# A decoder layer on one core: the turn of an attention step's output moved behind the next step's fourth scores

## The chip, the cores and the metric

The kernel runs on one core of a Trainium2 chip. The metric is the device time of one execution in microseconds (us); lower is better. A change of time is given against the kernel before.

## What is computed

One inference step of a one-layer decoder: a prompt of 512 tokens and 8 sample sequences of 8 tokens, model width 1024, in float32. The input projection gives q, k, v and two inputs of a convolution module. Attention has 8 heads of 64; the samples attend over a paged cache of 4096 keys each, in blocks of 256, of which the 3 with the highest mean score are taken besides the own one.

```python
z = h @ w_in + b_in
q, k, v, cva, cvg = jnp.split(z, [D_ATTN, 2 * D_ATTN, 3 * D_ATTN, 3 * D_ATTN + D_CV], axis=-1)
attn = moba_fn(q, k, v)
glu = cva * jax.nn.sigmoid(cvg)
c = _causal_dwconv(glu_ext, w_cv_dw, b_cv_dw)          # 31 taps
c = jax.nn.silu(_layernorm(c, g_cv_ln, b_cv_ln)) @ w_cv_pw + b_cv_pw
x = x + _rmsnorm(jnp.concatenate([attn, c], axis=-1) @ w_out, g_post_mix)
u = _causal_dwconv(ffn_hist + (_rmsnorm(x, g_pre_ffn) @ w_up), w_ffn_dw, b_ffn_dw)   # 3 taps
x = x + _rmsnorm((jax.nn.silu(gate) * val) @ w_down, g_post_ffn)
```

## The kernel before

Every engine runs its own instruction list, written out by hand in program order; semaphores join them. An engine never passes an instruction that waits, so the order in the code is the order on the engine.

After the input work the kernel goes through eight **steps**, b = 0 to 7, one for each sample sequence. A step has these parts, and the names are those of the code:

- **Scores.** `scores(b, j)`, j = 0 to 3, is TensorE's product of queries and a quarter of the keys (L520; the fourth also does the own keys, L532). The first two of a step run within the step before, behind its third and sixth `weigh`; the third and fourth stand at the head of the step. Each needs two tiles of keys that VectorE has turned (`turn_k`, L1372). ScalarE copies the scores out of the accumulator banks (`put_scores`, L1007), VectorE reduces them (`reduce_scores`, L1422 and L1423).
- **Softmax.** VectorE picks the blocks and adds the penalties (L1427 to L1456, among them L1435, L1439, L1442), ScalarE takes the exponentials (`exps`, L1013 and L1016).
- **The gap.** While VectorE and ScalarE do that, TensorE does other work: `glu_group` (L598) in steps 0 and 1, two tiles of the input projection in steps 2 to 4 (`TILES_IN`, `tile`, L611), statistics in step 5, nothing in step 6, `mix_half(1, ...)` of the output projection (L717) and `turn_history` (L728) in step 7.
- **Values.** `first_values` turns the probabilities (L553), then eight `weigh` (L574) multiply them with values that DMA brings; between these, `fill` puts more work of the projections and of the prompt's attention.
- **Output.** VectorE normalizes the step's output (`norm_out`, L1469 and L1473), which it can do only after the last `weigh`, and after everything that stands ahead of it in its own list, such as the turn of the next step's last keys and, in step 6, the rows of the residual (`mix_rows(0)`, L1534 to L1551). TensorE turns it (`turn_out`, L584), ScalarE copies it out (`put_out`, L1032). Only `turn_values`, `rows_out`, `first_values` and the end of the last step need that copy (semaphore `ot_put`).

Meanwhile ScalarE multiplies the taps of the 31-wide convolution (`taps`, L1072 and L1073), 24 in the eight `fill` of a step and up to 5 in its gap, and GpSimd adds each product to the sum (L1766). There are two product buffers, so neither gets far ahead. In step 7 ScalarE does a root, `row_root(0)` (L1208), at the head of the step; VectorE's `scale_rows(0)` (L1557, L1558) waits for it, and VectorE's scores of step 7 stand behind that.

Of the kernel before, what the change touches and what calls it, by code (L numbers as in the profile page):

```python
# [87 lines left out]
def build_layer(nc, a):  # L88
    ctx = ExitStack()
    with ctx:  # L90
# [361 lines left out]
        def _(pe):  # L452
# [359 lines left out]
            glu_group(0, 3)  # L812
            for b in range(NB):
                scores(b, 2)
                if b:
                    turn_out(b - 1)
                scores(b, 3)
                if b in (0, 1):
                    for n in range(4):
                        glu_group(2 * b + 1, n)  # L820
                if b in TILES_IN:
                    for x in TILES_IN[b]:
                        tile(x)
                    if b < 4:
                        turn_values(TILES_IN[b][0] // 2, b, True)
                if b == 4:
                    rows_out()
                if b == 5:
                    pe.wait_ge(s["o2_put"], 2)
                    statistics(conv, s["st1_done"], s["conv_done"], CT)  # L830
                if b == 7:
                    for n in range(4):
                        mix_half(1, n // 2, n % 2)
                    turn_history()
                if b in (2, 3):
                    pe.wait_ge(s["v2_home"], 2 * b - 2)
                if b == 7:
                    pe.wait_ge(s["hf_put"], 2)
                first_values(b)
                for u in range(SUPER):  # L840
                    weigh(b, u)
                    fill(b, u)
                    if b < NB - 1 and u in (2, 5):
                        scores(b + 1, u // 3)
# [110 lines left out]
        def _(act):  # L955
# [268 lines left out]
            for b in range(NB):  # L1224
                if b == 6:
                    roots_of_variance()
                put_scores(b, 2)
                if b:
                    put_out(b - 1)
                put_scores(b, 3)  # L1230
                if b in (0, 1):
                    gate_exp(2 * b + 1, 0)
                    gate_exp(2 * b + 1, 1)
                    taps(4)
                if b in TILES_IN:
                    taps(3)
                    put_tile(TILES_IN[b][0])
                    taps(2)
                if b == 5:
                    for half in range(2):  # L1240
                        act.wait_ge(s["st1_done"], half + 1)
                        act.activation(mu[:, half * HALF:(half + 1) * HALF], Z[half][:, 0:HALF], ACT.Copy,
                                       scale=1.0 / DA).then_inc(s["mu_put"], 1)
                if b == 7:
                    row_root(0)
                exps(b)
                if b in TILES_IN:
                    put_tile(TILES_IN[b][1])
                    if b < 4:
                        put_turned_value(TILES_IN[b][0] // 2)  # L1250
                if b == 4:
                    put_rows()
                    put_tails()
                if b == 7:
                    mix_squares(1)
                put_turned(b)
                if b < NB - 1:
                    spread_q(b + 1)
                for u in range(SUPER):
                    fill(b, u)  # L1260
                    if b < NB - 1 and u in (2, 5):
                        put_scores(b + 1, u // 3)
# [653 lines left out]
```

## Time and profile before

| | |
|---|---|
| time, median of 3 runs | 1134.69 us (1132.8 to 1135.31) |
| profiled execution: its time | 1133.18 us |
| profiled execution: its span | 1131.4 us |
| mean granted TensorE clock | 0.928 of full |
| busy: TensorE, VectorE, ScalarE, GpSimd | 964.3, 666.1, 443.9, 457.2 us |

The span is the profiled stretch from the first to the last instruction; the time is the same execution as the device measures it. Busy shares are a mean over stages that have different limits. The eight steps fill about 55 to 650 us, the feed-forward layer the rest.

### The profile page before, as it was taken

To read this page: it belongs to the slowest core of one execution; us is meant where nothing else is said; L and a number is where in the kernel's file an instruction comes from. 1 tells how busy PE (TensorE), PEld (TensorE's weight loads), DVE (VectorE), ACT (ScalarE), POOL (GpSimd) and SP (SyncE) were. 2 spreads that over 40 slices of the span, in tenths; PEclk is the share of its full clock that TensorE was granted. 3 is DMA by queue.
4 is the path that set the end of the run, shared out by engine and by line. 5 is a ranking of instruction groups with operands and counts; after the bars stand their busy time and mean duration, and the time that the engine had idled before them with its cause. 6 is when DMAs were issued, how large, how long until landed. Compare 5 with 4: busy or idle time off the path is not lost.

```text
span 1131.4 us, 19587 instructions
## 1 busy us (share of the span) xinstructions
PE 964.3 (85%) x7520; PEld 710.2 (63%) x7520; DVE 666.1 (59%) x928; ACT 443.9 (39%) x885; POOL 457.2 (40%) x408
## 2 busy tenths in 40 slices
PE   2498899787887695892988897999999999999995
PEld 1356675354453453552645557999999999767663
DVE  0758574554726456566444326988888888523214
ACT  1314655757656543434123213233333333224322
POOL 1002865839476432343000323555645655323440
PEclk9799998888899798997998898999999999999998
DMA  9688988979897765897871510322233231212222
GB/s 328 215 271 273 309 290 273 337 236 331 271 309 280 255 215 178 277 322 273 307 225 36 163 50 26 105 82 75 75 91 97 75 112 38 75 56 83 86 71 84
DMA packets 155207, 205.19 MB, mean 181 GB/s; under 512 B 10097, under 2 KB 75634, under 8 KB 155072
## 3 DMA queue, kind: packets, MB, share of 16 engines
q1 hardware_dynamic: 154619, 202.33, 54.2%
q10 hardware_dynamic: 495, 1.62, 0.5%
q8 instruction: 59, 0.97, 0.3%
q14 instruction: 34, 0.28, 0.1%
HBM read 198.59 MB, written 5.68 MB: 181 GB/s over the span
## 4 chain that ended last, share of the span: by engine, by line
PE 61%; DVE 13%; POOL 13%; ACT 7%; issue 4%; DMA 2%; POOLq 0%; SPq 0%; DVEq 0%; ACTq 0%
POOL conv L1766 10%; PE tp L857 6%; PE z L857 6%; PE sc L857 6%; PE z L717 4%; PE ob L857 3%; PE sm L857 3%; PE z L889 3%; PE ob L889 3%; PE tp L889 3%; PE z L598 2%; PE sc L520 2%; PE ob L574 2%; PE z L611 2%; DMA wk<-in_w_in 2%
## 5 line engine op out<-in xcount | busy, mean ns | idle before, releaser
L1766 POOL TENSOR_TENSOR conv<-conv,prod 128x576 f32<-128x576 f32 x120 | 170.3, 1419 | 106.4 <-ACT prod L1073 91.3
L1372 DVE STREAM_TRANSPOSE kT<-kN 128x2048 f32<-128x2048 f32 x64 | 145.4, 2295 | 29.0 <-PE sc L520 15.2
L1803 POOL TENSOR_TENSOR wulo<-wu,wuhi 128x2048 fp32r<-128x2048 f32 x22 | 102.6, 4662 | 24.4 <-ACT wuhi L1188 24.4
L1072 ACT ACTIVATE prod<-glu,consts 128x512 f32<-128x512 f32 x124 | 88.9, 717 | 47.7 <-POOL conv L1766 44.5
L1821 POOL TENSOR_TENSOR wdlo<-wd,wdhi 128x1024 fp32r<-128x1024 f32 x22 | 57.4, 2610 | 90.0 <-ACT wdhi L1303 90.0
L574 PE MATMUL ob<-vN,pT 128*32 128x128 f32 x2048 | 75.4, 296 | 15.4 <-DMA vN<-in_cache_v 15.3
L611 PE MATMUL z<-hT,wz 128*128 128x512 f32 x192 | 87.7, 613 | 0.0
L1698 DVE TENSOR_TENSOR cvo<-cvo,sg 128x576 f32<-128x576 f32 x22 | 85.0, 3862 | 0.0
L1673 DVE TENSOR_TENSOR fTlo<-fT,fThi 128x1152 fp32r<-128x1152 f32 x22 | 29.8, 1356 | 91.6 <-ACT fThi L1302 91.6
L574 PEld LDWEIGHTS ob<-vN,pT 128*32 128x32 f32 x2048 | 62.3, 143 | 30.7 <-DMA vN<-in_cache_v 16.8
L520 PE MATMUL sc<-kT,qS 128*32 128x256 f32 x1024 | 72.0, 429 | 5.4 <-DVE kT L1372 5.4
L1422 DVE TENSOR_REDUCE small<-S 128x8 f32<-128x512 f32 x32 | 21.6, 676 | 93.2 <-ACT S L1007 92.9
L1691 DVE SCALAR_TENSOR_TENSOR cvo<-ux,small,cvo 128x512 f32<-128x512 f32 x88 | 66.2, 752 | 3.1
L1799 POOL TENSOR_TENSOR h2lo<-h2raw,h2hi 128x512 fp32r<-128x512 f32 (+1 forms) x10 | 11.9, 1206 | 133.8 <-ACT h2hi L1215 133.8
L598 PE MATMUL z<-hT,wz 128*128 128x288 f32 x256 | 65.8, 416 | 0.0
L611 PEld LDWEIGHTS z<-hT,wz 128*128 128x128 f32 x192 | 37.1, 197 | 45.1 <-issue 44.8
L553 PE MATMUL tp<-consts,S 128*128 128x128 f32 x128 | 24.8, 358 | 42.9 <-issue 24.8
L1302 ACT ACTIVATE fThi<-fT 128x1152 fp32r<-128x1152 f32 x22 | 25.7, 1166 | 90.9 <-issue 86.6
L598 PEld LDWEIGHTS z<-hT,wz 128*128 128x128 f32 x256 | 49.0, 194 | 15.5 <-issue 2.1
L717 PE MATMUL z<-wo,hT 128*128 128x512 f32 x128 | 58.0, 605 | 0.0
L1839 POOL COPY last<-ux 128x2 f32<-128x2 f32 x44 | 9.7, 221 | 117.8 <-ACT ux L1286 117.8
L1777 POOL TENSOR_SCALAR pP<-pP,small 128x128 f32<-128x128 f32 (+3 forms) x32 | 34.1, 1083 | 54.1 <-DVE small L1515 54.1
(311 smaller groups left out, 2531.1 us busy)
## 6 DMA issues: line engine op xcount, KB each, us to landing
kN<-in_cache_k SPq DMA_DIRECT2D x256, 256.0 KB, 4.4
vN<-in_cache_v SPq DMA_DIRECT2D x256, 256.0 KB, 4.0
wu<-in_w_up SPq DMA_DIRECT2D x44, 512.0 KB, 4.6
wd<-in_w_down SPq DMA_DIRECT2D x22, 512.0 KB, 3.6
wz<-in_w_in SPq DMA_DIRECT2D x20, 512.0 KB, 6.6
wo<-in_w_out SPq DMA_DIRECT2D x1, 4096.0 KB, 14.2
wq<-in_w_in SPq DMA_DIRECT2D x1, 2048.0 KB, 15.1
wk<-in_w_in SPq DMA_DIRECT2D x1, 2048.0 KB, 19.8
```

Source lines behind the costliest of these rows:

```text
L520: ins = pe.matmul(bank[32 * h4:32 * h4 + 32, :].rearrange("p (a g k) -> p a g k", a=2, g=2)[:, :, g, :], qS[:, hc, :], kT[:, 2 * (j % 2):2 ...
L574: ins = pe.matmul(OB[32 * hp:32 * hp + 32, 0:P], w, vN[:, c % 4, i, hp * P:(hp + 1) * P], start=False, stop=(u == SUPER - 1 and i == 3))
L598: ins = pe.matmul(Z[half][:, 0:HALF], wz[:, i % 2, k, u, :], hT[:, k, half * HALF:(half + 1) * HALF], start=(k == 0), stop=(k == KC - 1))
L611: ins = pe.matmul(Z[x % 2][:, 0:TP_], wz[:, x // 2 % 2, k, x % 2, :], hT[:, k, 0:TP_], start=(k == 0), stop=(k == KC - 1))
L717: ins = pe.matmul(Z[nh][0:m, :], mixT[:, k, t * P:t * P + m], wo[:, k, nh * TP_:(nh + 1) * TP_], start=(k == 0), stop=(k == KC - 1))
L857: ins = pe.matmul(bank8[4 * (f % 2) + n][:, 0:HALF], w[:, k, u * P:(u + 1) * P], x[:, k, half * HALF:(half + 1) * HALF], start=(k == 0 and ...
L889: ins = pe.matmul(y_banks[nh][t][:, :], x[slot][:, k2, t * P:t * P + P], w[slot][:, k2, :], start=(kk == 0 and k2 == 0 and j == 0), stop=( ...
L1072: act.activation(dst[:, 0:TP_], glu[:, i, j:j + TP_], ACT.Copy, scale=w_cv[:, i, j:j + 1])
L1372: dve.transpose(kT[:, u % 4, :, :].rearrange("p c (i k) -> p i c k", i=4), kN[:, c % 3, :, :].rearrange("p i (c k) -> p i c k", k=32)).the ...
L1698: me3.then(dve.tensor_tensor(cvo[:, f % 2, 0, :], cvo[:, f % 2, 0, :], sg2[:, f % 2, :], ALU.mult))
L1766: ins = pool.tensor_tensor(conv[:, i, :], conv[:, i, :], prod[:, n % 2, :], ALU.add).then_inc(s["prod_used"], 1)
L1803: pool.tensor_tensor(wulo[f % 2][:, :, :], wu[f % 2][:, :, :, :].rearrange("p k u n -> p k (u n)"), wuhi[f % 2][:, :, :].bitcast(F32), ALU ...
```

## The change

`turn_out(b - 1)` moves on TensorE from between the third and the fourth scores to behind the fourth; in steps 1 to 4 it moves further, behind the first piece of the gap's work. ScalarE's `put_out(b - 1)` follows it. No instruction is added or taken away.

```diff
             for b in range(NB):
                 scores(b, 2)
-                if b:
+                scores(b, 3)
+                if b >= 5:
                     turn_out(b - 1)
-                scores(b, 3)
                 if b in (0, 1):
                     for n in range(4):
                         glu_group(2 * b + 1, n)
+                        if b and n == 0:
+                            turn_out(0)
                 if b in TILES_IN:
-                    for x in TILES_IN[b]:
-                        tile(x)
+                    tile(TILES_IN[b][0])
+                    turn_out(b - 1)
+                    tile(TILES_IN[b][1])
                     if b < 4:
                         turn_values(TILES_IN[b][0] // 2, b, True)
...
                 put_scores(b, 2)
-                if b:
+                put_scores(b, 3)
+                if b >= 5:
                     put_out(b - 1)
-                put_scores(b, 3)
                 if b in (0, 1):
                     gate_exp(2 * b + 1, 0)
+                    if b:
+                        put_out(0)
                     gate_exp(2 * b + 1, 1)
                     taps(4)
                 if b in TILES_IN:
                     taps(3)
                     put_tile(TILES_IN[b][0])
+                    put_out(b - 1)
                     taps(2)
```

TensorE's list at the head of step 7, as a piece of the difference; L584 is the turn of step 6's output, L717 the first of the gap's output projection:

```order
 L520 MATMUL sc<-kT,qS 32x2x128 [waits s_put,kt_ready]
 L520 MATMUL sc<-kT,qS 32x2x128 x15
-L584 MATMUL tp<-consts,oN 128x128 [waits o_norm]
 L520 MATMUL sc<-kT,qS 32x2x128 [waits s_put,kt_ready]
 L520 MATMUL sc<-kT,qS 32x2x128 x15
 L532 MATMUL sm<-kOwn,qS 32x64 x16
+L584 MATMUL tp<-consts,oN 128x128 [waits o_norm]
 L717 MATMUL z<-wo,hT 128x512 [waits t1_put]
 L717 MATMUL z<-wo,hT 128x512 x7
```

The turn, with its wait for the normalized output, now stands behind the fourth scores and still ahead of the projection.

ScalarE's list at the same place, before:

```order
L1203 ACTIVATE small<-small 128x1 [waits mo_sum]
L1007 ACTIVATE S<-sc 128x4x4x32 [waits scores_done]
L1032 ACTIVATE oT<-tp 128x128 [waits ot_done]
L1007 ACTIVATE S<-sc 128x4x4x32 [waits scores_done]
L1208 ACTIVATE small<-small 128x1 [waits x1_sq]
```

and of the change, where lines of ScalarE's code have a number higher by three:

```order
L1206 ACTIVATE small<-small 128x1 [waits mo_sum]
L1010 ACTIVATE S<-sc 128x4x4x32 [waits scores_done] x2
L1035 ACTIVATE oT<-tp 128x128 [waits ot_done]
L1211 ACTIVATE small<-small 128x1 [waits x1_sq]
```

The copy of the turned output now stands between the fourth scores' copy and the root, no longer ahead of that copy.

TensorE's list at the head of step 2, as a piece of the difference; the two groups of L611 are the gap's two tiles:

```order
 L520 MATMUL sc<-kT,qS 32x2x128 [waits s_put,kt_ready]
 L520 MATMUL sc<-kT,qS 32x2x128 x15
-L584 MATMUL tp<-consts,oN 128x128 [waits v2_home,o_norm]
 L520 MATMUL sc<-kT,qS 32x2x128 [waits s_put,kt_ready]
 L520 MATMUL sc<-kT,qS 32x2x128 x15
...
 L611 MATMUL z<-hT,wz 128x512 [waits z2_put,wz_full1]
 L611 MATMUL z<-hT,wz 128x512 x7
+L584 MATMUL tp<-consts,oN 128x128 [waits v2_home,o_norm]
 L611 MATMUL z<-hT,wz 128x512 [waits z2_put]
 L611 MATMUL z<-hT,wz 128x512 x7
```

Here the turn moved past the fourth scores and the first tile; steps 3 and 4 have the same. The lists of VectorE, GpSimd and SyncE are unchanged.

## Rows read from the trace of the kernel before

**Rows 1.** The page: the chain that ended last, shares by engine.

```profile
PE 61%; DVE 13%; POOL 13%; ACT 7%; issue 4%; DMA 2%; POOLq 0%; SPq 0%; DVEq 0%; ACTq 0%
```

**Rows 2.** Timeline, head of step 7: start us, us, engine line op; last idle before, releaser.

```profile
574.10 2.31 DVE L1372 STREAM_TRANSPOSE kT<-kN 128x2048 f32<-128x2048 f32 x1
...
579.25 1.91 PE L520 MATMUL sc<-kT,qS 128*32 128x256 f32 x32
...
585.08 0.35 DVE L1473 TENSOR_SCALAR oN<-ob,small 128x128 f32<-128x128 f32 x1
585.49 0.33 PE L584 MATMUL tp<-consts,oN 128*128 128x128 f32 x1 [4.33 <-DVE oN L1473]
585.75 3.48 PE L520 MATMUL sc<-kT,qS 128*32 128x256 f32 x32
585.85 0.28 ACT L1032 ACTIVATE oT<-tp 128x128 f32<-128x128 f32 x1 [3.54 <-PE tp L584]
...
589.27 1.09 ACT L1007 ACTIVATE S<-sc 128x512 f32<-128x512 f32 x1 [3.14 <-PE sc L520]
589.74 14.00 PE L717 MATMUL z<-wo,hT 128*128 128x512 f32 x32
590.16 0.25 ACT L1208 ACTIVATE small<-small 128x1 f32<-128x1 f32 x1
590.45 0.16 DVE L1557 RECIPROCAL small<-small 128x1 f32<-128x1 f32 x1 [5.01 <-ACT small L1208]
```

**Rows 3.** Chain that ended last, behind step 7's softmax: start us, us, what.

```profile
604.11 1.15 ACT t L1200 x4
...
717.26 6.40 PE tp L857 x48
```

**Rows 4.** Timeline, head of step 2.

```profile
210.44 2.31 DVE L1372 STREAM_TRANSPOSE kT<-kN 128x2048 f32<-128x2048 f32 x1
...
213.24 0.47 PE L584 MATMUL tp<-consts,oN 128*128 128x128 f32 x1 [5.08 <-DVE oN L1473]
...
217.36 1.08 ACT L1007 ACTIVATE S<-sc 128x512 f32<-128x512 f32 x1
...
218.23 0.32 ACT L1032 ACTIVATE oT<-tp 128x128 f32<-128x128 f32 x1
218.44 1.09 ACT L1007 ACTIVATE S<-sc 128x512 f32<-128x512 f32 x1
```

**Rows 5.** Timeline of GpSimd alone, gap of step 2.

```profile
220.32 4.50 POOL L1766 TENSOR_TENSOR conv<-conv,prod 128x576 f32<-128x576 f32 x3 [0.74 <-ACT prod L1073]
226.53 2.94 POOL L1766 TENSOR_TENSOR conv<-conv,prod 128x576 f32<-128x576 f32 x2 [1.71 <-ACT prod L1073]
```

**Rows 6.** Chain that ended last, gap of step 2.

```profile
222.05 3.06 DVE rank L1435 x2
...
226.66 1.32 DVE small L1442
```

**Rows 7.** Chain that ended last, steps 1, 5 and 6.

```profile
156.03 0.77 DVE rank L1435 x2
...
158.34 0.19 DVE small L1442
...
431.53 0.26 PE tp L584
...
439.48 4.32 DVE small L1442
...
506.12 3.75 DVE sd L1633
```

**Rows 8.** Stretches: busy us of PE, PEld, DVE, ACT, POOL; then clock, DMA share, GB/s.

```profile
586.40:589.00 2.60, 2.60 (x30) 1.33 (x26) 0.00 (x0) 0.00 (x0) 0.00 (x0) 0.50 0.07 9
...
302.70:309.50 6.80, 6.62 (x56) 5.47 (x57) 4.63 (x3) 5.43 (x13) 1.06 (x1) 0.50 0.38 127
```

**Rows 9.** Timeline of TensorE, `first_values` of step 3.

```profile
301.39 1.09 PE L553 MATMUL tp<-consts,S 128*128 128x128 f32 x8 [3.88 <-ACT vP L1054]
```

## The prediction

> **What bounds the kernel now.** I read the page first: TensorE is 61% of the chain that ended last, VectorE and GpSimd 13% each [rows 1]. That says little of a move inside a step, so I then followed the chain of work in order of time from 55 to 650 us, to see which engine carries it at the head of each step, and read the timelines there. The question at each head is the same: is anybody on the chain waiting for the fourth scores, which the turn of the output holds up?
>
> In step 7 the answer is yes. The last keys are turned by 576.4 us (574.10 + 2.31), and the third scores end at 581.16. The fourth could start then. In place of that TensorE stands 4.33 us at the turn, because VectorE normalizes the output only at 585.08. The fourth scores run from 585.75 and take 3.48 us where the third took 1.91. ScalarE copies them at 589.27, does the root L1208 at 590.16, and VectorE, idle for 5.01 us, goes on at 590.45 with what the root gives; its softmax stands behind that [rows 2]. Each of these is on the chain.
>
> In steps 2 to 4 the answer is no. TensorE waits for the output there too, 5.08 us in step 2, but nearly all of that it would wait for the keys anyhow: they are ready at 212.75 (210.44 + 2.31), 0.5 us before the turn. And ScalarE copies the third scores only at 217.36 and the fourth at 218.44, since it is held by the taps, at GpSimd's pace; the copy of the turned output sits between the two, at 218.23 [rows 4]. So the chain runs from GpSimd's sums over the third scores' copy to VectorE, and VectorE's reductions of the third scores cover the copy of the fourth. The timelines of steps 3 and 4 read the same, two repeats of the pattern.
>
> **Step 7, the main term.** Removed from the chain is what lies between the normalized output and the root. The turn goes on at 585.49 as before, since neither VectorE's list nor its inputs change; its copy starts at 585.85 and takes 0.28. The fourth scores now run at 581.2, take 1.9 us, and with the own keys end before 584; ScalarE copies them (1.09) by about 584.3, so it waits at the turned output as before. The root, third in line, comes right behind that copy. By the row of the root itself, which starts 0.20 us before its predecessor's 1.09 us run out (589.27 + 1.09 = 590.36 against 590.16), it would start at 585.85 + 0.28 - 0.2 = 585.95 to 586.1, where it started at 590.16. That is 4.1 to 4.2 us [rows 2].
>
> Does the second input keep up? The output projection in the gap, 14.00 us, starts at 589.74 now. It would start behind the turn, at 585.8, so 3.95 us earlier, and ends at 599.8. ScalarE's squares of its rows (L1200) start behind the exponentials; on the chain they stand at 604.11, so they would be ready for it at 599.9 [rows 2, 3]. The two shift by the same amount within 0.2 us. Should the clock be down, the projection is late. Today the granted clock is 0.50 of 2.4 GHz, its level of 1.2 GHz, during most of the fourth scores' 3.48 us [rows 2, 8]; the same 3.5 us over the projection would lose half of it, 1.7 us, and leave 2.5 us of the 4.2. Today 4.33 us of idleness lie ahead of that stretch; afterwards the wait is from 583.6 to 585.49, about 1.9 us, so the lower clock is less likely.
>
> Behind the gap everything hangs on engines, not on a fixed transfer: the chain goes over the squares, the history, `weigh` and the projections, and at 717.26 it is TensorE's up-projection without a break [rows 3]. The values for the first four `weigh` were issued before 583 us, the later ones are issued as `weigh` frees their buffers, and move along. The first load of up-weights waits for the own keys' scores and starts some 6 us earlier, into a stretch with free DMA. I let the gain through whole: **4.2 us**.
>
> **Steps 2 to 4.** ScalarE's copy of the turned output leaves its place between the two score copies: 218.44 - 218.23, some 0.2 us [rows 4]. The next taps start that much earlier, and GpSimd's three sums with them; they run 220.32 to 224.82 [rows 5]. VectorE's L1435, the pair, ends at 225.11, 0.3 us behind them, and takes 3.06 where the pair takes 0.77 in step 1 [rows 7]; L1442 ends at 227.98, when GpSimd's next sum ends (226.53 + half of 2.94 = 228.0) [rows 5, 6]. So VectorE's softmax is tied to GpSimd's sums and follows them. The second tie goes by the tile: the fourth scores start 0.87 us earlier, partly at the lower clock, the first tile ends 0.5 to 0.6 us earlier, ScalarE copies it, then does the moved copy (0.32 - 0.1), then the taps: a net 0.2 to 0.4 earlier. Gain per step 0.2 to 0.4, for three steps 0.6 to 1.2. I take 0.2 to 0.3 each, **0.7 us**, since the start of `first_values` and the tile behind it, both at the lower clock, pass on less than the whole.
>
> The moved turn itself costs 0.3 us of TensorE behind the first tile. It is hidden: TensorE is idle 3.88 us ahead of step 3's `first_values` [rows 9]. Without that cover it would be 0.3 us a step. `turn_values` waits for the copy and for the second tile; the copy is 7 us older.
>
> **Steps 1, 5, 6: nothing.** In step 1 VectorE's reduction of the fourth scores does not wait for its copy. In step 5 the chain does go over the turn, 0.26 us [rows 7], and that comes off; but VectorE's L1442 takes 4.32 us there where it takes 0.19 in step 1, until GpSimd's subtraction of the mean has ended, and this starts as before, with the statistics. The 0.26 us vanish in it. In step 6 VectorE does a 3.75 us reciprocal from 506.12 on [rows 7], while the fourth scores' copy is made in time.
>
> For L1442 the Trainium skill has a rule (SBUF — State Buffer, Who interferes with whom): VectorE's `tensor_scalar` in a two-port mode and GpSimd take one shared pair of ports, and the later one blocks until the other has finished. By the rule step 5 gains nothing; if VectorE were only slow in itself there, 0.26 us more would come off the sum. The row agrees with the rule: 4.32 us against 0.19.
>
> **Sum.** 4.2 + 0.7 = 4.9; less 0.4 for the chance (about one in four) that the projection loses 1.7 us to the clock: 4.5 us. Against the profiled execution's own 1133.18 us that is 1128.7. It lies 1.5 us below the median of the three runs; a median should come out at 1134.69 - 4.5 = **1130.2 us**. What a measurement of this kernel can tell from no change is about 0.2%, 2.3 us.
>
> **Rivals.**
> *The gain of step 7 is cut.* The clock is down during the projection, or the softmax is late for another reason, and 2.5 us remain; steps 2 to 4 give nothing, because the clock takes there what the copies give. For it speaks that `first_values` of step 3 starts at the full clock after 3.88 us of idleness and falls to 0.50 from 302.7 to 309.5 [rows 8, 9]; with 0.5 us more idleness ahead it may start at 0.50, which costs about half of the eight's 1.9 us. Time: 1134.69 - 2.5 + 0.9 = 1133.1.
> *No change at all.* The 4.2 us are given back behind step 7, at a transfer or another engine. Against it: from 617 us on no wait for a DMA stands on the chain. 1134.7.
> *Slower, by the clock.* Every moved wait changes the length of TensorE's pauses; if the lower clock covers more of the steps, each microsecond in it costs up to half a microsecond of TensorE. The stretch of step 3 is 6.8 us long [rows 8], up to 3.4 us of loss. Two such stretches more, in gaps that now run at the full clock, plus 3.4 us in the projection of step 7, cost 6.8 + 1.7 = 8.5 us against 4.9: 1138.3. It decides from about 10 us more at 0.50 on. Against it: no pause grows by more than 0.9 us, and the longest, in step 7, shrinks.
>
> On the clock the Trainium skill (TensorE: Matmul & The Clock Gate, HAM oscillation) says that waits of some length between bursts put the array back to half its clock, every time. By that rule a longer pause ahead of `first_values` speaks against the change, at up to 0.9 us in step 3, and the shorter one in step 7 for it, at 1.6 us. The trace shows both levels at these places.
>
> **Chances and range.** The forecast (gain of 3.3 to 6) 0.68; the cut gain (1 to 3.3) 0.17; no change 0.10; slower by the clock 0.05. The ends of the unknowns are 4.2 + 1.2 = 5.4 us and 2.5 - 0.9 = 1.6 us; with 1.2 us of spread as in the three runs, 1127.9 to 1133.2. Faster by over 0.2%: the forecast and most of the cut gain's upper half, some 0.78; within 0.2%: 0.17; slower: 0.05.
>
> **What the new profile would show.** At step 7's head the fourth scores right behind the third, 1.9 us for 32; the turn behind a wait of about 1.9 us; the root 0.1 us behind the turned output's copy and VectorE waiting for it under 1 us, not 5.01; the chain no longer over L520 between L584 and L1208; the projection's 32 in 14.0 us. At steps 2 to 4: ScalarE's two score copies back to back, L1435 and L1442 as long as before and 0.2 to 0.4 us earlier. Steps 5 and 6 unchanged, L1442 shorter by just the 0.26. Wrong it would be if the root still came late, if the distance from the root to `weigh` grew, or if the stretches at 0.50 grew by several microseconds.

## The result: 5 us faster, below the forecast range

The changed kernel takes 1127.15 us (median of 11 runs, 1124.76 to 1131.32). The kernel before, in 11 runs that belong to the same comparison (the three shown ahead of the prediction are among them), takes 1132.64 (1129.43 to 1135.31). The ratio is 0.9958, its 95% interval 0.9942 to 0.9974: a gain of 0.42%, 4.8 us of 1132.64 (2.9 to 6.6). The forecast was a gain of 4.5 us and a time of 1130.2, with a range from 1127.9. The gain came as forecast; the time lies 0.75 us below the range. Among the experiments further down two single executions ran far slower than all others, one of 3165.55 us of all_but_step7 and one of 1197.8 us of behind_first_piece; the medians of these two kernels count them, the ratios leave them out.

The profiled execution took 1130.34 us, span 1128.5 us, mean granted clock 0.931 (before: 1133.18, 1131.4 and 0.928).

The first part of the page to look at is the chain that ended last, which answers to [rows 1]:

```profile
PE 62%; DVE 13%; POOL 13%; ACT 7%; issue 3%; DMA 2%; POOLq 0%; SPq 0%; DVEq 0%; ACTq 0%
```

It can't tell the two kernels apart. The head of step 7 can. This is its timeline in the changed kernel, the piece that answers to [rows 2] (start us, us, engine line op; last the idle time before and its releaser). The numbers of TensorE's lines shown here are the same, ScalarE's have grown by 3, VectorE's and GpSimd's by 6:

```profile
579.79 3.64 PE L520 MATMUL sc<-kT,qS 128*32 128x256 f32 x64
...
583.49 1.10 ACT L1010 ACTIVATE S<-sc 128x512 f32<-128x512 f32 x1 [0.54 <-PE sc L520]
...
585.62 0.35 DVE L1479 TENSOR_SCALAR oN<-ob,small 128x128 f32<-128x128 f32 x1
...
586.02 0.33 PE L584 MATMUL tp<-consts,oN 128*128 128x128 f32 x1 [2.15 <-DVE oN L1479]
...
586.39 0.28 ACT L1035 ACTIVATE oT<-tp 128x128 f32<-128x128 f32 x1 [1.79 <-PE tp L584]
586.56 0.28 ACT L1211 ACTIVATE small<-small 128x1 f32<-128x1 f32 x1
...
586.88 0.16 DVE L1563 RECIPROCAL small<-small 128x1 f32<-128x1 f32 x1 [0.91 <-ACT small L1211]
```

The reader is to see three things. The third and fourth scores run as one group of 64 in 3.64 us, 32 in 1.8. TensorE still waits for the normalized output, but 2.15 us and not 4.33, and behind the scores. And the root L1211 comes 0.17 us behind the start of the turned output's copy, with VectorE waiting 0.91 us for it and not 5.01.

The two profiles are 0.54 us apart when the third scores start (579.25 and 579.79), so times are compared from there. The root starts 10.91 us behind that point before and 6.77 us now: **4.14 us earlier**.

What stands behind the root is less good. First the chain that ended last in the changed kernel (start us, us, what), then two stretches (busy us of PE, PEld, DVE, ACT, POOL; then clock, DMA share, GB/s) and TensorE's timeline at the projection's start:

```profile
586.02 0.33 PE tp L584
586.35 15.45 PE z L717 x32
...
601.82 0.69 ACT t L1203 x2
```

```profile
587.00:590.20 3.20, 3.20 (x5) 1.21 (x5) 3.13 (x6) 1.15 (x1) 0.00 (x0) 0.54 0.82 142
590.20:602.00 11.80, 11.80 (x32) 5.06 (x31) 7.80 (x25) 3.86 (x11) 0.00 (x0) 1.00 0.18 52
```

```profile
586.19 2.42 PE L717 MATMUL z<-wo,hT 128*128 128x512 f32 x3
```

From the turn to the squares the chain no longer goes over the softmax; it goes over the whole output projection. By TensorE's timeline this took 14.00 us before and takes 15.60 now (586.19 to 601.79): for 3.2 us the granted clock is 0.54, nearly its lower level of 1.2 GHz, and the first three matmuls need 0.81 us each. ScalarE's last squares end at 602.51 on the chain (601.82 + 0.69), 22.72 us behind the third scores' start. Before they end at 605.26 [rows 3], 26.01 us behind it. So the step gains **3.3 us** of the root's 4.14.

How long each step is can be read from one row per step, ScalarE's copy of the turned probabilities `pTo` (L1028; L1031 in the changed kernel). The changed kernel has it here for steps 6 and 7:

```profile
529.34 0.36 ACT L1031 ACTIVATE pTo<-sm 64x256 f32<-64x256 f32 x1
...
613.63 0.36 ACT L1031 ACTIVATE pTo<-sm 64x256 f32<-64x256 f32 x1
```

The distance is 84.29 us. The table gives these distances for all profiles; "step n" is the distance from the copy of step n-1 to that of step n.

| profile | step 1 | 2 | 3 | 4 | 5 | 6 | 7 |
|---|---|---|---|---|---|---|---|
| before | 61.0 | 68.4 | 64.9 | 69.3 | 78.9 | 75.3 | 87.5 |
| changed | 58.5 | 72.3 | 63.2 | 69.9 | 78.7 | 75.5 | 84.3 |
| only_step7 | 58.8 | 67.8 | 64.7 | 69.3 | 78.9 | 75.3 | 84.3 |
| all_but_step7 | 60.1 | 69.2 | 66.5 | 67.4 | 78.9 | 75.6 | 87.6 |
| norm_first | 60.5 | 68.9 | 65.0 | 69.4 | 78.9 | 75.3 | 82.1 |
| behind_first_piece | 60.3 | 66.3 | 65.0 | 69.0 | 78.8 | 75.6 | 82.1 |
| five_taps | 58.4 | 72.4 | 64.8 | 69.1 | 81.4 | 75.5 | 84.3 |
| direct_everywhere | 59.5 | 66.4 | 64.9 | 69.4 | 81.6 | 75.5 | 84.3 |
| step7_piece_only | 60.5 | 68.3 | 65.3 | 69.3 | 78.9 | 75.3 | 82.1 |
| norm_first_copy_behind | 61.0 | 68.8 | 65.0 | 69.3 | 78.9 | 75.3 | 82.1 |
| changed_again | 60.4 | 68.8 | 65.0 | 69.0 | 78.8 | 75.6 | 84.3 |
| norm_first_again | 61.1 | 69.4 | 63.8 | 69.5 | 79.0 | 75.3 | 82.1 |
| taps_behind | 60.5 | 67.3 | 64.2 | 68.8 | 78.7 | 75.5 | 84.3 |

Step 7 takes three values, 87.5, 84.3 and 82.1, and each is the same to 0.1 us in every profile of its kind. Steps 1 to 4 differ by up to 3.5 us between two executions of one and the same kernel (changed and changed_again, step 2), so a gain of tenths there can't be read from single profiles. From the last copy to the end of the span it is 515.0 us before (1131.4 - 616.38) and 514.9 in the changed kernel (1128.5 - 613.63): there nothing is given back behind step 7. In the five profiles in which step 7 takes 82.1 us it is 515.3 to 515.4, so some 0.4 us come back there.

Now steps 2 to 4. The chain in the gap of step 2, changed kernel, which answers to [rows 6] (L1441 was L1435, L1445 was L1439, L1448 was L1442), and GpSimd's timeline beside it, which answers to [rows 5]:

```profile
222.90 2.93 DVE rank L1441 x2
225.85 3.07 DVE rank L1445 x2
...
229.66 0.19 DVE small L1448
```

```profile
221.02 7.60 POOL L1772 TENSOR_TENSOR conv<-conv,prod 128x576 f32<-128x576 f32 x5 [0.59 <-ACT prod L1076]
```

Before, GpSimd made three sums, stood idle 1.71 us and made two more. Now it makes five without a break, since the first tile is copied out early enough for ScalarE's next taps. VectorE's two rank pairs both stand in that stretch, and each takes 3 us where it takes 0.8 without a sum beside it. The forecast had only L1441 wait. L1448 is free in return: 0.19 us where L1442 took 1.32. From the start of the first pair to the end of L1448 it is 6.95 us where it was 5.93, so 1.0 more. In step 5 the chain goes over the scores as one group, without the turn between them, and L1448 is hardly longer than before (4.32 us [rows 7]):

```profile
430.22 3.63 PE sc L520 x64
...
439.63 4.37 DVE small L1448
```

### The profile page after: what moved, and what is told of

Its sections match the earlier page's. It is cut to its first block, busy times and chain, and to the rows that moved or that the text cites. A ratio compares the mean times of both kernels' runs of the same rounds, so it can differ in the third digit from the quotient of the medians.

```text
span 1128.5 us, 19587 instructions
## 1 busy us (share of the span) xinstructions
PE 959.1 (85%) x7520; PEld 708.5 (63%) x7520; DVE 670.4 (59%) x928; ACT 444.7 (39%) x885; POOL 459.9 (41%) x408
## 4 chain that ended last, share of the span: by engine, by line
PE 62%; DVE 13%; POOL 13%; ACT 7%; issue 3%; DMA 2%; POOLq 0%; SPq 0%; DVEq 0%; ACTq 0%
POOL conv L1772 10%; PE tp L860 6%; PE z L860 6%; PE sc L860 6%; PE z L717 5%; PE ob L860 3%; PE sm L860 3%; PE z L892 3%; PE ob L892 3%; PE tp L892 3%; PE z L598 2%; PE sc L520 2%; PE z L611 2%; PE ob L574 2%; DMA wk<-in_w_in 2%
## 5 line engine op out<-in xcount | busy, mean ns | idle before, releaser
L1704 DVE TENSOR_TENSOR cvo<-cvo,sg 128x576 f32<-128x576 f32 x22 | 93.8, 4265 | 0.0
L574 PE MATMUL ob<-vN,pT 128*32 128x128 f32 x2048 | 74.4, 293 | 17.2 <-DMA vN<-in_cache_v 17.2
L611 PE MATMUL z<-hT,wz 128*128 128x512 f32 x192 | 86.8, 606 | 0.0
L574 PEld LDWEIGHTS ob<-vN,pT 128*32 128x32 f32 x2048 | 61.4, 142 | 32.3 <-DMA vN<-in_cache_v 19.3
L520 PE MATMUL sc<-kT,qS 128*32 128x256 f32 x1024 | 67.9, 413 | 11.2 <-DVE kT L1378 11.2
L611 PEld LDWEIGHTS z<-hT,wz 128*128 128x128 f32 x192 | 36.2, 194 | 43.6 <-issue 43.4
L717 PE MATMUL z<-wo,hT 128*128 128x512 f32 x128 | 59.6, 619 | 0.0
L520 PEld LDWEIGHTS sc<-kT,qS 128*32 128x32 f32 x1024 | 34.0, 118 | 38.5 <-issue 12.0
```

The lines of the kernel that those rows point to most:

```text
L520: ins = pe.matmul(bank[32 * h4:32 * h4 + 32, :].rearrange("p (a g k) -> p a g k", a=2, g=2)[:, :, g, :], qS[:, hc, :], kT[:, 2 * (j % 2):2 ...
L574: ins = pe.matmul(OB[32 * hp:32 * hp + 32, 0:P], w, vN[:, c % 4, i, hp * P:(hp + 1) * P], start=False, stop=(u == SUPER - 1 and i == 3))
L611: ins = pe.matmul(Z[x % 2][:, 0:TP_], wz[:, x // 2 % 2, k, x % 2, :], hT[:, k, 0:TP_], start=(k == 0), stop=(k == KC - 1))
L717: ins = pe.matmul(Z[nh][0:m, :], mixT[:, k, t * P:t * P + m], wo[:, k, nh * TP_:(nh + 1) * TP_], start=(k == 0), stop=(k == KC - 1))
L1704: me3.then(dve.tensor_tensor(cvo[:, f % 2, 0, :], cvo[:, f % 2, 0, :], sg2[:, f % 2, :], ALU.mult))
```

## The experiments

Theory A, from the trace: the whole gain is step 7's; of it the root gives 4.1 us and the lower clock over the projection takes 0.8 back. Its rival B: steps 2 to 4 give a part as forecast, and it is only not seen in single profiles. Eleven runs followed, ten of nine edited kernels and one of the changed kernel again; all ratios are to the kernel before on the same chip.

### The two halves of the change

**only_step7**: the change in step 7 alone.

```diff
                 scores(b, 2)
-                if b:
+                if 1 <= b < 7:
                     turn_out(b - 1)
                 scores(b, 3)
+                if b == 7:
+                    turn_out(b - 1)
```

(and the same for `put_out` on ScalarE.)

> The kernel before with the turn of step 6's output alone moved behind step 7's fourth scores; steps 1 to 6 as before. Theory (the gain is step 7's): 3.2 to 4.2 us faster than before, ratio 0.9963 to 0.9972, and within 1 us of the whole change; VectorE's wait for the root under 1 us, the projection in the gap on the chain if the clock is down. Rival (the gain is in steps 1 to 4, step 7 is given back later): within 1 us of before.

**all_but_step7**: the changed kernel, with step 7 as before.

```diff
                 scores(b, 2)
+                if b == 7:
+                    turn_out(b - 1)
                 scores(b, 3)
-                if b >= 5:
+                if b in (5, 6):
                     turn_out(b - 1)
```

(and the same for `put_out` on ScalarE.)

> The whole change except step 7, whose turn stays between third and fourth scores. Theory: steps 2 to 4 give between 1 us and nothing, since GpSimd's sums block VectorE's L1439 for some 2.3 us whenever the first tile ends before ScalarE asks for it, and give 0.2 to 0.4 us when it doesn't: ratio 0.999 to 1.001. Rival: 2 to 4 us faster, ratio 0.9965 to 0.998.

Measured: only_step7 1128.61 us (12 runs), ratio 0.9965 (0.9951 to 0.998); all_but_step7 1132.53 us (12 runs), ratio 0.9999 (0.9987 to 1.0011); the kernel before 1133.17 (29 runs). Theory A holds. The moves of steps 1 to 6 together are worth nothing that can be measured; by the interval it is at most 1.5 us of gain and at most 1.2 of loss.

### The wait at the turn, and the projection's clock

If the projection loses 1.6 us because TensorE stands at the turn just ahead of it, then a kernel in which it doesn't stand there should reach more than the change. Two ways: make the output ready earlier, or put work ahead of the turn.

**norm_first**: the kernel before, with all turns in their old places; VectorE alone normalizes step 6's output ahead of the residual's rows.

```diff
-                    elif u == 7:
-                        mix_rows(0)
...
                 norm_out(b)
+                if b == 6:
+                    mix_rows(0)
```

> The kernel before with another edit: VectorE normalizes step 6's output ahead of the residual rows mix_rows(0) and no longer behind them; the turn stays between third and fourth scores. If the turn's wait for the normalized output is the cause, this alone removes it: 4.0 to 4.6 us faster than before (ratio 0.996), the turn without a wait, the projection starting near 584 and not on the chain. If it was only the place of the turn or of its copy that cost (the rival), nothing changes.

Measured: 1126.73 us (6 runs), ratio 0.9946 (0.9928 to 0.9963); and again on another chip, as norm_first_again:

> VectorE normalizes step 6's output ahead of the residual's rows, all turns where they stood before; once more, beside the changed kernel on the same chip. If the two microseconds of step 7 by which it is ahead in the profiles (82.1 against 84.3) are real, it comes out at 0.994 to 0.995 of the kernel before and 1.5 to 2 us under the changed kernel. If they are lost in later waits, the two are equal within 0.7 us.

1127.04 us (6 runs), ratio 0.9946 (0.9925 to 0.9968). The timeline of norm_first_again at the head of step 7, and the stretch of the projection in which the changed kernel has the clock at 0.54:

```profile
579.73 1.91 PE L520 MATMUL sc<-kT,qS 128*32 128x256 f32 x32
...
580.19 0.35 DVE L1473 TENSOR_SCALAR oN<-ob,small 128x128 f32<-128x128 f32 x1
...
581.57 0.33 PE L584 MATMUL tp<-consts,oN 128*128 128x128 f32 x1
...
581.83 1.93 PE L520 MATMUL sc<-kT,qS 128*32 128x256 f32 x32
...
584.14 8.42 PE L717 MATMUL z<-wo,hT 128*128 128x512 f32 x19
...
585.48 0.29 ACT L1208 ACTIVATE small<-small 128x1 f32<-128x1 f32 x1 [0.52 <-DVE t L1551]
```

```profile
587.00:590.20 3.20, 3.20 (x8) 1.34 (x8) 3.01 (x8) 0.07 (x1) 0.00 (x0) 1.00 0.95 174
```

The turn finds its input ready, TensorE doesn't pause at all, the clock stays full, and the projection starts 2 us earlier than in the changed kernel. The root waits for VectorE's squares (0.52 us), no longer for ScalarE. From the third scores' start to the root it is 5.75 us, 1.0 less than in the changed kernel, and the step is 2.2 us shorter. The turn's old place between the scores, the one that the change gives up, costs 0.2 us when its input is ready: the fourth scores start 2.10 us behind the third, which take 1.91. More came than I had expected (0.996): the root alone is 5.16 us earlier than in the kernel before (10.91 less 5.75), where I had expected 4.0 to 4.6 for the whole.

Where the changed kernel loses its 2.2 us against norm_first_again can be read from three distances. The root comes 1.0 us later. From the root to the end of the projection's squares it is 15.95 us in the changed kernel (586.56 to 602.51), but 15.15 here (585.48 to 600.63) and 15.10 in the kernel before, which both have the projection at 14.00 us: 0.8 more. From these squares to the copy of the probabilities it is 11.12 and 10.75 us: 0.4 more.

**behind_first_piece**: the changed kernel, with step 7's turn behind the first quarter of the projection and its copy behind the root.

```diff
                 scores(b, 3)
-                if b >= 5:
+                if b in (5, 6):
                     turn_out(b - 1)
...
                     for n in range(4):
                         mix_half(1, n // 2, n % 2)
+                        if n == 0:
+                            turn_out(b - 1)
...
                 if b == 7:
                     row_root(0)
+                    put_out(b - 1)
```

> The changed kernel, and in step 7 the turn goes behind the first quarter of the projection and its copy behind the root. TensorE no longer stands still for the normalized output, and the root follows the sum of squares directly. Theory: the root 1.0 us earlier and the projection 1.8 us earlier than in the changed kernel, so 1 to 2.5 us faster than it, 5.5 to 7 us faster than before (ratio 0.994 to 0.995). Rival (something behind step 7 takes over): no faster than the changed kernel.

**step7_piece_only**: the same edit of step 7 in the kernel before, the other steps as they were.

```diff
                 scores(b, 2)
-                if b:
+                if 1 <= b < 7:
                     turn_out(b - 1)
...
                         mix_half(1, n // 2, n % 2)
+                        if n == 0:
+                            turn_out(b - 1)
...
                     row_root(0)
+                    put_out(b - 1)
```

> The kernel before, and in step 7 alone the turn goes behind the first quarter of the projection and its copy behind the root; steps 1 to 6 as before. Theory (step 7 is all of it, and the moves in steps 1 to 4 are worth nothing): 5 to 6 us faster than before, ratio 0.9945 to 0.9955, and no slower than the same step 7 with the moves of steps 1 to 6 (0.9956). Rival (steps 1 to 6 give about 1 us): 0.9965.

Measured: behind_first_piece 1127.65 us (12 runs), ratio 0.9956 (0.9938 to 0.9973); step7_piece_only 1126.92 us (6 runs), ratio 0.9947 (0.9932 to 0.9961). Both have step 7 at 82.1 us, 5.4 less than before. The first one's ratio misses the expected 0.994 to 0.995 and is hardly below the changed kernel's; its interval reaches over both. In both kernels VectorE's list is that of the changed kernel and only TensorE's pause is gone: their clock is 1.00 over the projection's first 3.5 us.

**norm_first_copy_behind**: norm_first, and ScalarE's `put_out` behind the fourth scores' copy in every step, with TensorE's turns left in place.

```diff
                 put_scores(b, 2)
+                put_scores(b, 3)
                 if b:
                     put_out(b - 1)
-                put_scores(b, 3)
```

> The kernel with the normalization ahead of the residual rows, and ScalarE's copy of the turned output moved behind the fourth scores' copy in every step; TensorE's list as before. Theory of the prediction for steps 2 to 4 (the copy's slot of 0.2 us a step comes off the chain through taps and sums): 0.2 us less in each of the three steps, at most 0.6 us in all, so ratio 0.994 to 0.9947, which the interval can't tell from 0.9946; in the profile VectorE's L1435 pair ends 0.2 us earlier behind the third scores' copy. Rival: nothing moves.

Measured: 1128.81 us (6 runs), ratio 0.9961 (0.9947 to 0.9975), step 7 again 82.1. The ratio misses the expected 0.994 to 0.9947, though its interval overlaps norm_first's. Taking the copy out from between the scores' copies gives steps 2 to 4 nothing: they are 68.8, 65.0 and 69.3 us, against 68.9, 65.0 and 69.4 in norm_first. But the edit doesn't test what it was made for. The copy still stands ahead of the taps here, and they start 2.04 us behind the start of the third scores' copy, 1.96 in norm_first. In the changed kernel it stands behind three taps and the tile's copy. Its taps start 1.82 us behind the third scores' copy (1.81 in changed_again), where the kernel before has 1.96: there the slot is freed, by 0.15 us.

**changed_again**: the changed kernel a second time.

> The changed kernel once more, for a second profile and a second set of times. If the gain is as measured (0.9958), it repeats within 0.0015. Where the lower clock falls is the open point: if it falls on the projection of step 7 in every execution, the distance from step 7's root to the copy of its turned probabilities is again near 27.1 us and the 32 matmuls take about 15.6 us; if it was the luck of one execution, they take 14.0 and the distance is about 26.0. The pair of rank operations in steps 2 and 4 takes 3.06 us again if GpSimd's earlier sums block it by the order alone, and 0.76 in some step if it is a matter of tenths.

Measured: 1128.78 us (12 runs), ratio 0.9963 (0.9948 to 0.9979). Step 7 is 84.31 us and the root stands 27.07 us ahead of the copy of the probabilities, both as in the first profile, so the loss to the clock is no luck of one execution: the 32 matmuls take 15.60 us again. It is there in all six profiles in which TensorE waits at the turn behind the fourth scores (changed, changed_again, only_step7, five_taps, direct_everywhere, taps_behind), and in none of the five in which it doesn't. In the other two (before, all_but_step7) TensorE stands at the turn between the scores, and it is the fourth scores that are slow, 3.48 and 3.43 us.

### The gaps of steps 2 to 4

**direct_everywhere**: the changed kernel, with the turn and its copy directly behind the fourth scores in steps 1 to 4 too.

```diff
                 scores(b, 3)
-                if b >= 5:
+                if b:
                     turn_out(b - 1)
...
                     tile(TILES_IN[b][0])
-                    turn_out(b - 1)
                     tile(TILES_IN[b][1])
```

> The changed kernel, but in steps 1 to 4 the turn and its copy stand directly behind the fourth scores and not behind the first piece of the gap. Theory: steps 1 to 4 give nothing that can be told either way, ratio to before 0.9955 to 0.9965, as the changed kernel and as the kernel with step 7 alone. Rival (the place behind the first piece matters): 1 us or more off the changed kernel.

Measured: 1129.31 us (12 runs), ratio 0.9975 (0.9962 to 0.9988). Expected was 0.9955 to 0.9965; the edge is missed by 1.1 us, and the interval reaches into it. The second rank pair (L1439 here) is blocked in step 4 alone.

**five_taps**: the changed kernel, with all five taps of the gap ahead of the tile's copy, so that GpSimd has sums to make for as long as VectorE ranks.

```diff
-                    taps(3)
+                    taps(5)
                     put_tile(TILES_IN[b][0])
                     put_out(b - 1)
-                    taps(2)
```

> The changed kernel, and in the gaps of steps 2 to 4 ScalarE does all five taps together ahead of the first tile's copy, so GpSimd's five sums run without a pause. Theory (sums without a pause block VectorE's L1439 pair behind the L1435 pair): the L1439 pair takes near 3 us in all three steps where it takes 0.77 unblocked; L1442 is free in return, so each step loses 1 to 2 us against an unblocked one, and the kernel is 1 to 3 us slower than the changed one, ratio to before 0.997 to 0.9985. Rival (the placing of the sums doesn't matter): as the changed kernel, 0.9958.

Measured: 1133.63 us (12 runs), ratio 1.0007 (0.9997 to 1.0018). I had expected 0.997 to 0.9985. The whole gain of step 7 is gone, though that step is 84.3 us in it as well. The rank pair L1444 is blocked in all three steps; here step 2, from the chain:

```profile
222.06 2.95 DVE rank L1440 x2
225.04 3.07 DVE rank L1444 x2
```

But the theory that each blocked pair makes its step 1 to 2 us longer isn't borne out by the profile. Steps 3 and 4 are 64.8 and 69.1 us with the pair blocked, and 65.0 and 69.0 in changed_again with it free. What the profile has more than that of changed_again stands in steps 1 and 2 together (130.8 us against 129.1) and in step 5 (81.4 against 78.8), which is looked at below. That five sums without a pause are slower is measured; that the blocked pair is the reason is shown for at most a part of it.

**taps_behind**: the opposite; the gap's last two taps behind the exponentials.

```diff
                     put_tile(TILES_IN[b][0])
                     put_out(b - 1)
-                    taps(2)
...
                 exps(b)
                 if b in TILES_IN:
                     put_tile(TILES_IN[b][1])
+                    taps(2)
```

> The changed kernel, but the last two taps of the gap in steps 2 to 4 stand behind the exponentials on ScalarE. If it is GpSimd's sums that block VectorE's rank pair there (3.06 us against 0.76), the pair is short in at least two of the three steps and the steps shorten by up to 2 us each, time 0.991 to 0.9945. If the two sums are only put off and hold up ScalarE's and GpSimd's work during the values, the steps keep their length and the time stays at 0.9955 to 0.998, with the pair short all the same.

Measured: 1128.97 us (12 runs, 1126.36 to 1134.28), ratio 0.9975 (0.9956 to 0.9994). Its timeline of VectorE and of GpSimd in step 2:

```profile
219.67 2.94 DVE L1441 TENSOR_TENSOR rank<-small 128x256 f32<-128x256 f32 x2
222.64 0.76 DVE L1445 TENSOR_TENSOR rank<-rank,consts 128x256 f32<-128x256 f32 x2
...
224.16 0.18 DVE L1448 TENSOR_SCALAR small<-small 128x32 f32<-128x32 f32 x1
```

```profile
217.82 4.51 POOL L1772 TENSOR_TENSOR conv<-conv,prod 128x576 f32<-128x576 f32 x3 [0.61 <-ACT prod L1076]
```

The three sums end at 222.33, the pair L1445 starts at 222.64 and is free, in step 2 as in 3 and 4. So it is GpSimd's sums that block it. The second half of the expectation is what the times say: the sums are put off and not gone, and no gain over the changed kernel can be measured. The profiled run, 1126.57, was one of its fastest, so the short steps 2 and 3 of its row in the table don't stand for its median.

How close this is to chance is seen in the second profile of the changed kernel, where the pair is free (the chain of step 2, then GpSimd's timeline):

```profile
223.39 2.91 DVE rank L1441 x2
226.32 0.77 DVE rank L1445 x2
...
227.84 0.71 DVE small L1448
```

```profile
221.51 4.50 POOL L1772 TENSOR_TENSOR conv<-conv,prod 128x576 f32<-128x576 f32 x3 [0.60 <-ACT prod L1076]
227.09 2.95 POOL L1772 TENSOR_TENSOR conv<-conv,prod 128x576 f32<-128x576 f32 x2 [1.08 <-ACT prod L1076]
```

In both profiles L1441 starts 1.88 us behind GpSimd's group. What differs is further up, at the fourth scores of step 2. This is TensorE's timeline, of the first profile and of the second:

```profile
213.67 1.93 PE L520 MATMUL sc<-kT,qS 128*32 128x256 f32 x32 [1.73 <-DVE kT L1378]
```

```profile
214.16 3.28 PE L520 MATMUL sc<-kT,qS 128*32 128x256 f32 x32 [1.99 <-DVE kT L1378]
```

The first has the full clock, the second most of the way the lower one. So in the first the tile behind the scores is done sooner, its copy too, GpSimd's fourth sum starts without a pause and stands in the pair's way; in the second ScalarE waits for the tile, GpSimd pauses 1.08 us, and the pair slips through. The step with the faster scores is 3.5 us the longer one (72.3 and 68.8). Of these 3.5 us the softmax explains 1.8: from the start of L1441 to the end of L1448 it is 6.95 us and 5.16, since the pair pays 2.3 and L1448 gets 0.5 back. Another 1.9 us lie ahead of the third scores' copy and have nothing to do with the pair: the copy of step 1's probabilities, from which the step is counted, is 2.4 us earlier in the first profile (169.87 and 172.27), but the third scores' copy, which the chain reaches over a long row of GpSimd's sums, only 0.5 us (218.31 and 218.79). Some 0.2 us come back behind the softmax.

Nor does it take the change to get there. norm_first and norm_first_again are one kernel, with the turns of steps 2 to 4 in their old places, and their two profiles differ in step 2 in the same way. With the fourth scores at 1.93 us the five sums have no break and the second pair takes 3.06 us; with the scores at 3.38 us GpSimd pauses 1.39 us and the pair takes 0.77. The step is 69.4 us and 68.9: only 0.5 us longer with the pair blocked.

### A second spread, in step 5

direct_everywhere and five_taps have step 5 at 81.4 to 81.6 us where all others have 78.7 to 79.0. The distance covers the values of step 4, and there the chains of the kernel before and of five_taps read the same up to one piece:

```profile
397.59 2.19 PE sc L520 x32
399.78 0.87 PE ob L574 x32
400.65 2.30 PE sc L682 x8
```

```profile
398.10 3.56 PE sc L520 x32
401.65 0.87 PE ob L574 x32
402.53 2.30 PE sc L682 x8
```

The granted clock over the 4 us from there is 0.91 before (397.5 to 401.5) and 0.56 in five_taps (398 to 402). The scores lose 1.4 us. direct_everywhere has them at 3.57 us on its chain too, and the eleven profiles with a short step 5 have the group at 2.2 to 2.4 us. The other microsecond is for the most part a second slow stretch: by TensorE's timeline the second `weigh` behind these scores (L574, at 408.34 and 407.42) takes 1.94 us in these two, and 1.11 in changed_again. What makes the clock fall there was not tried.

## Why the prediction was right, and where it was wrong

- **What bounds the kernel.** Right. Someone waits for the fourth scores in step 7; elsewhere nobody does in a way that shows: only_step7 has the gain (0.9965), all_but_step7 has none that can be measured (0.9999).
- **The root, 4.1 to 4.2 us earlier.** Right: 4.14 us. The step "its copy starts at 585.85 and takes 0.28", with the root "right behind that copy", holds to 0.1 us.
- **Does the projection keep up?** The case that I gave one in four is what happens. The step that failed is "afterwards the wait is from 583.6 to 585.49, about 1.9 us, so the lower clock is less likely". The wait was 2.15 us and the lower clock came in six profiles of six. Its size was half right: the projection takes 1.60 us more, as priced (1.7), but the step loses only 0.85 us (27.07 against 26.22 from the root to the copy of the probabilities), because the projection had been ahead of ScalarE and used that up first: it ended at 603.74 [rows 2], and the second pair of squares that needs it began only about 604.7, half way through the four of [rows 3]. That the two numbers differ by about that lead (0.75 us) is worked out from the rows; that the loss is 0.8 to 0.85 is also what the distances from the root to the squares give (15.95 us with the slow projection, 15.10 and 15.15 with the fast one). I had set it off whole. One of my signs of being wrong was "if the distance from the root to `weigh` grew", and it did, by this. With 0.85 the term is 3.3 us, where the forecast had 4.2 less 0.4.
- **Steps 2 to 4, 0.7 us.** Not found. The interval of all_but_step7 has room for 0.7 us, but no profile shows it. The first tie is right as far as it goes: in step 2 the first pair ends 0.15 us nearer to the third scores' copy (7.66 us from its start before, 7.52 and 7.51 in the two profiles of the changed kernel). The step that failed is "So VectorE's softmax is tied to GpSimd's sums and follows them". Each rank pair, and not only the first, is tied to the sum that runs when it starts. A tile that is copied earlier moves GpSimd's next sum over the second pair, which then takes 3.07 us in place of 0.77; the shorter L1448 gives 0.5 to 1.1 of this back. Whether that happens is a matter of tenths and of the clock over the fourth scores, as the two profiles of norm_first show, and so differs between two executions of one kernel by more than the change could give.
- **Steps 5 and 6, nothing.** Right in the sum, wrong in how. The step that failed is "The 0.26 us vanish in it". From the start of the third scores to the end of L1442 it is 14.13 us before (429.67 to 443.80) and 13.78 in the changed kernel (430.22 to 444.00): GpSimd's subtraction comes earlier too, since the statistics on TensorE that it waits for stand behind the same scores. But steps 5 and 6 together are 154.2 us in both; the 0.35 us are given back among the values of the two steps. Where, was not tried.
- **The shared port.** The Trainium skill (SBUF — State Buffer, Who interferes with whom) says that a VectorE operation with two inputs in SBUF also contends with a GpSimd operation that reads there, and that the order of issue decides who blocks. The profiles agree: a rank pair takes 2.9 to 3.1 us where a sum runs as it starts, and 0.77 where none does. I had used the page for L1442 only, when it bore as much on the two rank pairs.
- **Behind step 7 the gain goes through whole.** Right: 515.0 and 514.9 us.
- **The sum.** By profile the gain is 3.3 us in step 7 and nothing elsewhere; by the times it is 4.8 (2.9 to 6.6) and, the second time, 4.2 (2.4 to 5.9). The 3.3 lies in both intervals. That the forecast of 4.5 is nearer to the medians is then partly luck: by the profiles one term was too large by 0.5, one by 0.7.
- **The time.** This is the step that put the result outside the range: "a median should come out at 1134.69 - 4.5". The base was a median of three runs. The medians of larger sets are 1132.64, 1133.17, 1132.99 and 1133.10 us (11, 29, 23 and 23 runs), 1.5 to 2 us lower. The profiled execution, 1133.18, was nearer to them, and I named it and went by the other. And the spread of 1.2 us "as in the three runs" is too small: single runs of the kernel before lie from 1128.09 to 1135.46. The range's ends do not follow from its terms either: 1134.69 - 5.4 - 1.2 is 1128.1 and 1134.69 - 1.6 + 1.2 is 1134.3, where I wrote 1127.9 and 1133.2. With a base of 1133.1 and the same gain, 1128.6 would have been the forecast; the two medians of the changed kernel are 1127.15 and 1128.78.
- **The rivals.** The cut gain of step 7 came in its mechanism, not in its size. Its other half, the clock in steps 2 to 4, came as well: `first_values` of step 3 stands behind 3.94 us of idleness, where it was 3.88, and starts at the lower clock in both profiles of the changed kernel. From its start to the turns of the own keys' probabilities (L556) it is 3.69 us, where it was 3.23. But that needs no change of these steps: norm_first_again has 3.69 as well, behind 3.89 us, and norm_first 3.23, behind the same 3.89. "No change at all" is out by the gain. A slowing by the clock did not come: the mean granted clock is 0.928 before, 0.931 and 0.925 in the two profiles of the changed kernel.

A better edit than the change is norm_first, 0.9946 twice: it removes the cause (VectorE makes the output late), where the change moves the instruction that waits for it. step7_piece_only does as well, 0.9947. Their lead over the changed kernel is 2.2 us in step 7 in every profile, of which 0.4 are given back behind it; by the ratios it is 1.2 to 1.9 us, and the intervals overlap.

## What to carry to other kernels

When an instruction waits for a late input and work stands behind it, ask first whether the producer can be earlier, and only then where the waiter may stand: moved, it still pauses its engine, and the next long stretch of matmuls may pay with its clock. When two engines block each other, a gain of tenths ahead of them is worth nothing until it is known which operation the next start falls on. And a forecast of a time needs a base with a spread as wide as that of many runs, not of three; forecast the gain, and add it to the middle of everything that is known of the base, the profiled run included.

## What was not expected of the hardware

- The lower clock behind a pause of only 2.15 us. TensorE had been busy at the full clock with the scores and the own keys up to 583.87 (583.24 + 0.63) and stood until 586.02; from 587.0 to 590.2 the granted clock is 0.54, and from 590.2 on 1.00. Without a pause there (norm_first) it is 1.00 over the same stretch. step7_piece_only, which has VectorE's list unchanged and only TensorE's pause removed, has 1.00 there too. What else the fall hangs on stays open. The same kernel in step 2 shows both levels behind pauses that differ by 0.26 us (1.73 and 1.99).
- A faster stretch can make a step longer: with the fourth scores of step 2 at the full clock, GpSimd's sums close up, the pair behind them pays 2.3 us, and the softmax as a whole is 1.8 us longer (1.5 in the two profiles of norm_first).
